# Half-array products taken in turn, and the first fill of five weight places begun by halves

## The reference, cut to what matters

```python
def nsa_compress(kv, pe, w1, w2):
    ...
    blocks = blocks.transpose(0, 1, 3, 2, 4).reshape(B, n_c, G, NSA_CMP_LEN * D)
    return jax.nn.silu(blocks @ w1) @ w2          # 2048 -> 64 -> 64, for keys and for values
...
    s = jnp.einsum("btgjd,bcgd->bgjtc", qb, kc) * scale      # six heads x 15 blocks
```

```python
    t_inv = lax.linalg.triangular_solve(eye + a_mat, ..., unit_diagonal=True)
    u = t_inv @ (vc * bc[..., None])
    w = t_inv @ (kb * jnp.exp(gcum)[..., None])
    ...
    hid = jax.nn.silu(jnp.einsum("becd,edf->becf", xe, w_gate)) * jnp.einsum("becd,edf->becf", xe, w_up)
    ye = jnp.einsum("becf,efd->becd", hid, w_down) * gate[..., None].astype(h.dtype)
```

## Time and profile before

| what | value |
|---|---|
| timed runs (3) | 1213.13 us median, 1210.08 to 1213.62 |
| the profiled execution's own time | 1207.15 us |
| its span, first to last instruction | 1205.4 us |
| mean granted TensorE clock | 0.951 of full speed |
| TensorE busy | 1033.0 us (86%) |
| moved by DMA | 323.69 MB, mean 269 GB/s |

### The profile page before, as it was taken

The page is one execution under the profiler, slowest core; times in us unless marked ns, Lnnn a source line. Parts: engine busy times, 40 slices in busy tenths (PEclk is TensorE's granted clock), DMA queues, the critical chain, the costliest instruction groups (busy, mean ns, idle before and its releaser), DMA issues.

```text
span 1205.4 us, 18371 instructions
## 1 busy us (share of the span) xinstructions
PE 1033.0 (86%) x7810; PEld 541.0 (45%) x7810; DVE 435.3 (36%) x1031; ACT 240.4 (20%) x590; POOL 55.1 (5%) x70
## 2 busy tenths in 40 slices
PE   5999999999999989999998889898675666766666
PEld 2345764444577446885676765432111111211111
DVE  0138646423855527345348773411000000000002
ACT  0012144111213513445112251200000000000002
POOL 0101000000100000001212400000000000000000
PEclk9999999999989999999999999899989888879789
DMA  9963348443325984013322015999999999999996
GB/s 385 411 268 140 117 148 334 171 157 140 140 88 233 429 367 157 1 70 147 134 73 73 4 71 217 418 407 433 428 428 432 430 429 431 429 428 430 430 431 281
DMA packets 28160, 323.69 MB, mean 269 GB/s; under 512 B 3264, under 2 KB 3392, under 8 KB 5808
## 3 DMA queue, kind: packets, MB, share of 16 engines
q1 hardware_dynamic: 26048, 314.18, 63.6%
q0 software_dynamic: 2032, 8.35, 1.9%
HBM read 321.47 MB, written 1.05 MB: 268 GB/s over the span
## 4 chain that ended last, share of the span: by engine, by line
PE 58%; DMA 33%; DVE 5%; issue 2%; SPq 1%; ACT 1%; DVEq 0%; ACTq 0%
PE banks L650 48%; DMA ring<-in_stream 17%; DMA zuv_to_Kt<-in_stream 15%; PE banks L661 3%; PE banks L913 1%; SPq L553 1%; PE banks L934 1%; PE banks L2219 1%; PE banks L899 1%; PE banks L896 1%; PE banks L800 1%; DVE KC L1249 0%; PE banks L904 0%; PE banks L937 0%; DVE probs L1299 0%
## 5 line engine op out<-in xcount | busy, mean ns | idle before, releaser
L650 PE MATMUL banks<-ring,uT 128*128 128x512 f32 (+1 forms) x512 | 225.8, 595 | 7.3 <-DVE uT L1116 3.0
L650 PEld LDWEIGHTS banks<-ring,uT 128*128 128x128 f32 x512 | 96.3, 192 | 121.1 <-issue 114.0
L650 PE MATMUL banks<-scr_qk 64*64 64x64 f32 (+4 forms) x2368 | 97.3, 266 | 25.8 <-DMA scr_qk<-in_stream 19.0
L650 PE MATMUL banks<-ring,scr_qk 128*32 128x512 f32 (+1 forms) x496 | 85.1, 642 | 28.4 <-DMA ring<-in_stream 27.7
L2790 DVE SCALAR_TENSOR_TENSOR UWK<-UWK,banks 128x256 f32<-128x256 f32 x16 | 6.7, 421 | 263.8 <-ACT UWK L3076 263.8
L650 PE MATMUL banks<-ring,UWK 128*32 128x512 f32 (+1 forms) x336 | 85.4, 768 | 12.8 <-ACT UWK L3084 9.2
L650 PEld LDWEIGHTS banks<-scr_qk 64*64 64x64 f32 (+3 forms) x2368 | 70.0, 135 | 54.3 <-issue 41.8
L3076 ACT ACTIVATE UWK<-banks 128x256 f32<-128x256 f32 x16 | 6.1, 384 | 361.1 <-PE banks L650 361.1
L650 PE MATMUL banks<-UWK,ring 128*128 128x256 f32 x320 | 71.0, 380 | 0.0
L2219 PE MATMUL banks<-UWK 128*128 128x512 f32 x128 | 65.3, 633 | 0.9 <-DVE UWK L2798 0.9
L650 PEld LDWEIGHTS banks<-UWK,ring 128*128 128x128 f32 x320 | 60.4, 190 | 9.3 <-issue 1.4
(11 more groups left out here) (384 smaller groups left out, 1223.4 us busy)
## 6 DMA issues: line engine op xcount, KB each, us to landing
ring<-in_stream SPq DMA_DIRECT2D x93, 2048.0 KB, 14.7
scr_qk<-in_stream SPq DMA_DIRECT2D x11, 2048.0 KB, 40.0
Vt_to_O<-in_stream SPq DMA_DIRECT2D x11, 2048.0 KB, 39.5
zuv_to_Kt<-in_stream SPq DMA_DIRECT2D x10, 2048.0 KB, 39.2
scr_qk<-in_stream SPq DMA_DIRECT2D x11, 1024.0 KB, 41.2
wide<-in_stream SPq DMA_DIRECT2D x10, 1024.0 KB, 38.8
const<-in_stream SPq DMA_DIRECT2D x10, 1024.0 KB, 37.5
misc<-in_stream SPq DMA_DIRECT2D x10, 1024.0 KB, 39.4
```

The source lines that it names most:

```text
L650: return pe.matmul(o, a, b, start=start, stop=stop)
```

## The change: what it does

Four edits.

1. `pe_cmp1` takes the products of v = 0 and v = 1 in turn. Those of v = 1 now go to output partitions 64 to 127 of bank 3, so the two use different column halves of the array; `hid` for v = 1 sits in those partitions too. Both banks are waited for ahead of the first product, and both results are announced at the end.
2. `pe_cmp_s` takes products of the lower and the upper 64 partitions in turn; both banks are waited for at the start.
3. The W products take the lower and upper 64 partitions in turn.
4. SP's list for the first fill of the expert places is written out. Five units (3, 4, 6, 7 and, in other positions, 8 and 9, which were already two halves) go by halves of 1 MB, each half behind the last reader of its own memory. The first halves of units 6 and 7 wait for a new event, `y2_half`, that TensorE raises when it has read the first half of an output weight for the second tile.

```diff
-        parts[b] = parts.get(b, 0) + (2 if (b in SPLIT or k == first + PLACES) and k < len(order) - 1 else 1)
+        halved = b in SPLIT or k in (first + 4, first + 6, first + 7, first + PLACES)
+        parts[b] = parts.get(b, 0) + (2 if halved and k < len(order) - 1 else 1)
...
+            sp.wait_ge(*at("G_mm", 1, 1))
+            send(first + 2)
+            sp.wait_ge(*at("Z_mm", 1, 1, LEVELS - 1))
+            send_half(first + 9, 0)
+            sp.wait_ge(*at("W_mm", 1, 1, 1))
+            send_half(first + 3, 0)
+            sp.wait_ge(*at("KV_mm", 1, 2, 1))
+            send_half(first + 3, 1)
+            sp.wait_ge(*at("AV_mm", 3, 1))
+            send_half(first + 4, 0)
+            sp.wait_ge(*at("O", 3, 1))
+            send_half(first + 8, 1)
+            sp.wait_ge(*at("mix2", 1, 1))
+            send_half(first + 4, 1)
+            send(first + 5)
+            for i, event in enumerate(("y2_half", "y2_mm")):
+                for cg in range(2):
+                    sp.wait_ge(*at(event, cg, 1))
+                    send_half(first + 6 + cg, i)
+            sp.wait_ge(*at("h_lat", 1, 1))
+            send_half(first + 8, 0)
+            sp.wait_ge(*at("grow_mm", 1, 1))
+            send_half(first + 9, 1)
...
         def pe_cmp1(pe, l):
-            for v in range(2):
-                pe.wait_ge(*free(2 + v))
-                for a in range(LPAIR):
-                    ins = mm(pe, bank[2 + v][0:HD, 0:2 * N_CMP], w1[:, v, a, :],
+            pe.wait_ge(*free(2))
+            pe.wait_ge(*free(3))
+            for a in range(LPAIR):
+                for v in range(2):
+                    ins = mm(pe, bank[2 + v][HD * v:HD * v + HD, 0:2 * N_CMP], w1[:, v, a, :],
                              blk[:, v, a, :, :].rearrange("p g c -> p (g c)"), a == 0, a == LPAIR - 1)
...
         def pe_cmp_s(pe, l):
-            for b in range(2):
-                pe.wait_ge(*free(6 + b))
-                for h in range(b, NSA_H, 2):
-                    for t in range(TILES):
+            pe.wait_ge(*free(6))
+            pe.wait_ge(*free(7))
+            for i in range(NSA_H // 2):
+                for t in range(TILES):
+                    c = (i * TILES + t) * N_CMP
+                    for b in range(2):
...
-                for p in (0, CH):
-                    for i in range(NDH):
+                for i in range(NDH):
+                    for p in (0, CH):
                         ins = mm(pe, bank[4 * t + 2 + p // CH][:, i * CH:(i + 1) * CH], bK[p:p + CH, i * P:(i + 1) * P],
                                  scr[p:p + CH, t, TT_, i * CH:(i + 1) * CH], True, True)
...
+            elif t:
+                ins.then_inc(*tick("half_used", "y2_half", cg, t))
```

More of the change, by code:

```diff
@@ L523, in _, with send, send_half @@
             sp.dma_start(const[:, 0:C_FIRST], A["consts"][:, 0:C_FIRST]).then_inc(*tick("consts_in", "consts", 0, by=16))
-            for k in range(len(units)):
+            def send(k):
+                sp.dma_start(held(slot[k]), A["stream"][k, :, :]).then_inc(*tick(f"arrived{slot[k]}", by=16))
+            def send_half(k, i):
+                sem = "arrived_last" if (k, i) == (len(units) - 1, 1) else f"arrived{slot[k]}"
+                sp.dma_start(halves(slot[k])[i], A["stream"][k, :, i * HALF:(i + 1) * HALF]).then_inc(*tick(sem, by=16))
+            first = units.index(("gu_mm", 0, 0))
+            for k in range(first):
                 if k == 2:
@@ L546, in _ @@
[L546 to L551, removed]
+                if before[k] is not None:
+                    sp.wait_ge(*at(*units[before[k]]))
@@ new lines, in _ @@
+                send(k)
+            sp.wait_ge(*at("zuv_mm", 1, 1))
+            send(first)
+            sp.wait_ge(*at("zuv_mm", 0, 1))
+            send(first + 1)
+            sp.wait_ge(*at("G_mm", 1, 1))
[6 more added lines that the diff above has]
+            send_half(first + 3, 1)
@@ new lines, in _ @@
+            send_half(first + 8, 0)
+            sp.wait_ge(*at("grow_mm", 1, 1))
+            send_half(first + 9, 1)
+            for k in range(first + PLACES, len(units)):
+                if k == first + PLACES:
+                    sp.wait_ge(*at("gu_half"))
+                    send_half(k, 0)
+                    sp.wait_ge(*at("gu_mm", 0, 0))
+                    send_half(k, 1)
+                    continue
+                sp.wait_ge(*at(*units[before[k]]))
+                if slot[k] in SPLIT or k == len(units) - 1:
+                    send_half(k, 0)
+                    send_half(k, 1)
@@ L830, in pe_cmp1 @@
             pe.wait_ge(*at("blocks", l))
-            for v in range(2):
-                pe.wait_ge(*free(2 + v))
-                for a in range(LPAIR):
-                    ins = mm(pe, bank[2 + v][0:HD, 0:2 * N_CMP], w1[:, v, a, :],
+            pe.wait_ge(*free(2))
[3 more added lines that the diff above has]
+                    ins = mm(pe, bank[2 + v][HD * v:HD * v + HD, 0:2 * N_CMP], w1[:, v, a, :],
                              blk[:, v, a, :, :].rearrange("p g c -> p (g c)"), a == 0, a == LPAIR - 1)
-                ins.then_inc(*fill(2 + v, "cmp1", l, v))
+                    if a == LPAIR - 1:
+                        ins.then_inc(*fill(2 + v, "cmp1", l, v))
         def pe_cmp2(pe, l):
@@ L851, in pe_cmp_s @@
             pe.wait_ge(*at("turned", l, 5))
-            for b in range(2):
-                pe.wait_ge(*free(6 + b))
-                for h in range(b, NSA_H, 2):
-                    for t in range(TILES):
[L856 to L859, removed]
+            pe.wait_ge(*free(6))
[4 more added lines that the diff above has]
+                    for b in range(2):
+                        ins = mm(pe, bank[6 + b][:, c:c + N_CMP], TB[HD * b:HD * b + HD, B_NQ + i, t * P:(t + 1) * P],
+                                 KCT[HD * b:HD * b + HD, (2 * i + b) // HPG, :], True, True)
+                        if (i, t) == (NSA_H // 2 - 1, TILES - 1):
+                            ins.then_inc(*fill(6 + b, "cmp_s", l, b))
         def pe_cmp_pT(pe, l):
@@ L1591, in a_cmp_hid @@
                 act.wait_ge(*at("cmp1", l, v))
-                act.activation(hid[0:HD, v, :], bank[2 + v][0:HD, 0:2 * N_CMP], ACT.Tanh, scale=0.5).then_inc(*tick("scalar_step", "hid_tanh", l, v))
+                act.activation(hid[HD * v:HD * v + HD, v, :], bank[2 + v][HD * v:HD * v + HD, 0:2 * N_CMP], ACT.Tanh, scale=0.5).then_inc(*tick("scalar_step", "hid_tanh", l, v))
                 act.wait_ge(*last("scalar_step"))
```

23 lines of the change are left out of this document (5 added, 18 removed).

## The result

The changed kernel takes 1199.75 us (median of 6 runs, 1197.61 to 1204.55) against 1212.77 us for the kernel before (median of 6, 1210.08 to 1216.2). The ratio is 0.9898, 95% interval 0.9873 to 0.9922: 12.4 us less, between 9.5 and 15.4. Two executions of kernels made for the experiments took 2043 us (e7) and 4301 us (e8) and are in no ratio.

The account below looks back on a forecast made before the run. Expert-weight transfers after unit 13's issue were taken to bound the end, TensorE's chain setting that issue. W 4.9 + cmp_s 1.4 - cmp1 0.3 + fill 0 = 6.0 us gained: 1213.1 - 6.0 = 1207.1 us, range 1201 to 1213.5.

Parts of the forecast that it names:

- The bound: Expert-weight transfers at the end: the end moves only with unit 13's issue, which TensorE's list and short DVE waits set.
- The fill: SP's first fill: four halves (4.2 MB) go earlier but nothing waits for them; costed at 0, bounds 0 and 9.8 us.
- Rival (c): First fill counts in full, the queue being late, not dry, at 784 us: 15.8 us gained, 1197.3 us; chance 0.05.
- (a): Clock falls in the first layer too, slowing the projection behind cmp1 by 2.8 us: 3.2 us gained, 1209.9 us; chance 0.18.
- (d): Turns bring nothing anywhere and cmp1 pays for its wait: 4.0 us lost, 1217.1 us; chance 0.08.
- cmp1: All 64 products start after the DVE wait at 33 ns each: a loss of 0.3 us in two layers.
- rival (b): Column halves in cmp1 do not overlap, by the skill's rule: 2.3 us gained, 1210.8 us; chance 0.07.
- W and cmp_s: Turned products at 68 ns: W's 128 instructions save 4.9 us over two stages, cmp_s 1.4 us in two layers.
- the end of the sum: Gain of 6.0 us taken from the timed median 1213.1, not the profiled 1207.15 us, giving 1207.1 us; chance 0.62.

Follow-up runs that it names:

- e7: Changed kernel with the first six of eight pairs of W products computed twice: 1201.16 us, 0.9899 of the kernel before.
- e8: Kernel before, old order, with only five of eight W products of each half computed: 1206.2 us, ratio 0.9936.
- e2: Changed kernel with the old products, so only the new transfer list differs from the kernel before: 1214.2 us, ratio 1.0009.
- e14: The changed kernel once more, one profiled execution: 1198.31 us.
- e1: Kernel before with the three product edits (cmp1, cmp_s, W) and its old transfer list: 1198.95 us, ratio 0.9884.
- e18: The changed kernel again, run beside the one with repeated W products: 1200.13 us, 0.9894 of the kernel before.
- e4: Changed kernel with cmp1 as it was before: 1199.58 us, 0.9891 of the kernel before.
- e5: Kernel before with W turned and nothing else: 1203.82 us, ratio 0.9914.
- e9: The kernel before as it is, one more profiled execution: 1212.95 us.
- e12: Kernel before with W turned in the first stage alone: 1209.2 us, ratio 0.9951.
- e3: The changed kernel itself, run again: 1199.16 us, 0.9888 of the kernel before.
- e6: Kernel before with cmp_s turned and nothing else: 1210.57 us, ratio 0.9975.
- e11: Kernel before with W turned in the second stage alone: 1209.21 us, ratio 0.9967.

## Why the forecast was wrong, step by step

**The bound: right.** From unit 13's issue to the end it is 422.2 to 424.1 us in all 19 traces, whatever the kernel, while the issue moves from 792.37 (e2) to 773.15 us (e14). All of the gain lies ahead of it.

**The fill: right.** Costed at 0; e2 gives 1.0009, and e1 without it is as fast as after. Rival (c), the fill in full at 1197.3 us, came near the measured time by accident: its mechanism is refuted.

**Rivals (a) and (d).** (d), that taking turns brings nothing, falls with the 63 and 60 ns below. (a) was a fall at cmp1 in the first layer. It came in three of seven traces with the new cmp1 (after, e1, e18) and in four of twelve with the old one (e4, e5, e9, e12), so the traces do not make it the change's doing, and it was no good sign of the forecast being wrong.

**cmp1: right.** The block waits 2.37 us for DVE and then runs at 31 to 33 ns an instruction. I took the 33 ns from the G products and a loss of 0.3 us; e4 against e3 shows none that can be measured. What I had not foreseen is the second layer: a fall comes in the block in all seven traces with the new cmp1, and in or right behind it in six of twelve with the old. These kernels have no more half clock ahead of W for it (see "What stays open"). The Trainium skill, "TensorE: Matmul & The Clock Gate", section "The mechanism", has it that a weight load overlaps a running product only where the row group differs. The two halves of cmp1 differ in columns alone and go from 62 to 31 ns, so for them the measurement decides against this sentence of the page, and rival (b) falls. For W and cmp_s, where the row group does differ, the trace agrees with it.

**W and cmp_s, direct: a little small.** 68 ns from the state update was too high for products with 64 moving columns, as I had suspected: W takes 63, cmp_s 60. 5.6 and 1.8 us in place of 4.9 and 1.4.

**The step that failed** is the end of the sum: "The timed runs before have a median of 1213.13, 6.0 us above that execution. I expect the runs after to be of the same kind as these, so the forecast is 1213.1 - 6.0 = 1207.1 us." The 6.0 us between the profiled execution and the others were taken as something that the change leaves alone. They were mostly falls of the clock around W and ahead of it which the profiled execution had been spared: it has a granted clock of 1.00 in both windows around W above, and of the 77 later executions of before only two took 1207.15 us or less. So the W term, 4.9 us, was mis-sized: measured alone it is 10.4 us (7.3 to 13.6), 5.6 direct, some 2 in the clock behind it as the traces have it, and the rest within the interval. cmp_s, 1.4 us, is 3.0 (0.8 to 5.1). I had looked at the clock only for a loss, in rival (a), and said in passing that a shorter cmp_s "might keep the clock up"; the term for it in the sum was zero, and it is W, not cmp_s, that goes with less half clock: 124.7 us against 134.7, where cmp_s alone has 135.4.

**What stays open.** By the traces the new products gain 7.2 us directly and 1.9 through the clock behind W, and ahead of W the new-cmp_s kernels are low for 10 us against 15 (nine and ten traces), another 2.5 us. That is 11.6, the timed runs say 12.4 to 14.1 with intervals of 3 us. The mean clocks of the timed executions give an estimate of their own: 13.7 us less at half clock, at 0.49 us each, is 6.7 us at most, with the direct part 13.9. Whether the 2.5 us ahead of W are cmp_s's doing is not shown: single executions of one kernel differ by more (after is low there for 6.8 to 17.1 us), and e6, cmp_s alone, was low for 17.1. The form of cmp1 divides the traces as sharply (8.8 us ahead of W in seven with the new one, 15.4 in twelve with the old), and e4, with the old cmp1 and the new cmp_s, has 13.7; by the timed runs e4 is no slower than e3, so that isn't shown either. Nor was it tried to hold the clock up with the old order unchanged; that the old order brings falls on rests on their place (e11, e12), their number and the mean clocks, not on a run that takes the falls alone away.

## What to carry to other kernels

Where small products use part of the array's rows, put other rows in between; two in a row of each half do as well as one. When the time of the profiled execution isn't the median, look for what it was spared before you forecast: list every stretch of half clock in it, ask which are missing that other executions have, and take more than one profile of the kernel before where the clock may matter. An edit that speeds up a chain of small products on one half of the array can pay twice, once in its own length and once in clock.

## What was not expected of the hardware

Turned in pairs (two products, four instructions on each half, 128 columns of weights) the chain takes 5.94 us, turned singly 5.88, in the old order 8.62: the gain has all come at half the changes. Products that differ in the column half alone, with 64 columns of weights and 30 moving columns, run at 31 ns in turn and at 62 on one half. And 5.36 us more of work on TensorE's chain cost about 1 us of time; some 1.9 us of it came back in a stretch further on whose chain runs through POOL and DVE, the rest is open.
